# A hybrid decoder trunk on one Trainium2 core: query tiles ahead of the last gate tile, three half gate tiles in an attention's end, thirteen selection rounds moved

## The reference

```
h = RMSNorm(x) * (1 + scale) + shift              # scale, shift from c (adaLN)
z = h @ w_in                                      # all mixers' inputs and 4 x 1024 gate columns
A: gated convolution of width 3      D: sparse attention: an indexer scores all keys, each query
F: attention with forget biases         keeps its top 256, softmax over them with ALiBi
S: banded attention, window 128, sinks
y = sum over A, F, S, D of sigmoid(gate_n) * (branch_n @ w_branch_n)
x = x + g1 * RMSNorm(y @ w_o)
x = x + g2 * RMSNorm(SwiGLU(RMSNorm(x) ...))      # channel sub-layer
```

## Time and profile before

| | us |
|---|---|
| median of 3 runs | 1734.74 (1734.55 to 1738.4) |
| the profiled execution | 1735.29 |
| its span, first to last instruction | 1733.5 |
| PE busy | 1680.1 (97%) |
| DVE busy | 1055.2 (61%) |
| POOL busy | 822.4 (47%) |
| ACT busy | 613.3 (35%) |
| mean granted PE clock, share of full speed | 0.992 |

### The profile page before, as it was taken

One profiled execution on the slowest core, in us unless ns is written; L12 is line 12 of the kernel. 1 busy time (PEld: TensorE's weight loads), 2 busy tenths in 40 slices (PEclk: granted clock), 3 DMA queues, 4 the chain that ended last, 5 costly groups with the idle time before them and its releaser, 6 DMA issues.

```text
span 1733.5 us, 22877 instructions
## 1 busy us (share of the span) xinstructions
PE 1680.1 (97%) x8072; PEld 1397.3 (81%) x8072; DVE 1055.2 (61%) x1756; ACT 613.3 (35%) x1104; POOL 822.4 (47%) x537
## 2 busy tenths in 40 slices
PE   5999999999999999989999999999999999999997
PEld 4877878787888888879888888888888888888886
DVE  7745745556999999947486445843553454345337
ACT  5544336374222222246423455332223223222323
POOL 2421130102436565620288434675567656655755
PEclk9999999999999999999999999999999999999999
DMA  8131141010111111340575403120112012111205
GB/s 342 37 85 47 51 115 35 16 52 17 61 46 46 45 46 45 112 103 1 217 273 171 170 14 133 37 73 30 66 49 68 29 48 73 48 48 48 73 25 207
DMA packets 37455, 138.87 MB, mean 80 GB/s; under 512 B 4624, under 2 KB 4624, under 8 KB 37392
## 3 DMA queue, kind: packets, MB, share of 16 engines
q1 hardware_dynamic: 35152, 130.70, 21.7%
q0 software_dynamic: 2240, 7.34, 1.9%
HBM read 118.10 MB, written 13.63 MB: 76 GB/s over the span
## 4 chain that ended last, share of the span: by engine, by line
PE 68%; issue 11%; POOL 10%; DVE 4%; DMA 4%; ACT 2%; SPq 1%; POOLq 0%; ACTq 0%; DVEq 0%
PE ps L639 19%; PE ps L640 18%; PE ps L641 18%; POOL w_t L1713 5%; PE ps L863 4%; PE ps L842 2%; PE ps L766 1%; DMA raw<-in_w_ffn 1%; PE ps L767 1%; POOL w_f L1728 1%; DMA region_a<-in_x 1%; PE ps L670 1%; POOL raw L1731 1%; POOL slot_c L1713 1%; DVE region_c L1904 1%
## 5 line engine op out<-in xcount | busy, mean ns | idle before, releaser
L639 PE MATMUL ps<-h_t,w_t 128*128 128x512 f32 x1112 | 437.7, 394 | 3.3 <-DVE h_t L1896 1.6
L641 PE MATMUL ps<-h_t,w_t 128*128 128x512 f32 x1112 | 433.6, 390 | 0.0
L640 PE MATMUL ps<-h_t,w_t 128*128 128x512 f32 x1112 | 433.5, 390 | 0.0
L639 PEld LDWEIGHTS ps<-h_t,w_t 128*128 128x128 f32 x1112 | 209.4, 188 | 49.7 <-issue 5.5
L641 PEld LDWEIGHTS ps<-h_t,w_t 128*128 128x128 f32 x1112 | 209.1, 188 | 44.0
L640 PEld LDWEIGHTS ps<-h_t,w_t 128*128 128x128 f32 x1112 | 209.4, 188 | 42.8 <-issue 0.7
L1564 POOL TENSOR_TENSOR w_t<-raw,w_t 128x1280 fp32r<-128x1280 f32 (+1 forms) x50 | 145.9, 2918 | 198.2 <-ACT w_t L1154 197.9
L2265 DVE TENSOR_TENSOR y_f<-ps,y_f 128x512 f32<-128x512 f32 x120 | 80.7, 686 | 217.5 <-PE ps L641 217.5
L1713 POOL TENSOR_TENSOR w_t<-raw,w_t 128x512 fp32r<-128x512 f32 x80 | 110.2, 1383 | 136.7 <-ACT w_t L1452 136.7
L1950 DVE MAX8 top<-region_b 128x8 f32<-128x384 f32 (+5 forms) x192 | 157.9, 882 | 17.6 <-issue 17.0
L1953 DVE MATCH_REPLACE8 region_b<-top,region_b 128x384 f32<-128x384 f32 (+5 forms) x192 | 166.1, 876 | 0.0
(11 more groups left out here) (286 smaller groups left out, 3345.4 us busy)
## 6 DMA issues: line engine op xcount, KB each, us to landing
raw<-in_w_ffn SPq DMA_DIRECT2D x46, 512.0 KB, 3.9
raw<-in_w_gates SPq DMA_DIRECT2D x32, 640.0 KB, 3.9
region_b<-in_w_ada SPq DMA_DIRECT2D x33, 512.0 KB, 4.5
region_d<-in_w_ffn SPq DMA_DIRECT2D x20, 512.0 KB, 4.0
raw<-in_w_z SPq DMA_DIRECT2D x18, 512.0 KB, 3.4
region_a<-in_x SPq DMA_DIRECT2D x8, 512.0 KB, 14.9
h_f<-in_w_ada SPq DMA_DIRECT2D x8, 512.0 KB, 8.1
raw<-in_w_o SPq DMA_DIRECT2D x8, 512.0 KB, 3.6
```

The source lines that it names most:

```text
L639: pe.matmul(o, a_hi, m_hi, start=first, stop=False, skip_group_check=more)
L640: pe.matmul(o, a_hi, m_lo, start=False, stop=False, skip_group_check=more)
L641: return pe.matmul(o, a_lo, m_hi, start=False, stop=last, skip_group_check=more)
```

## The change

Four things are changed; what is computed stays the same.

1. `T_DSA` moves one place ahead. The order is now 23 gate tiles, the two query tiles, the last gate tile of branch S (`T_LAST`), the sparse attention. The queries' stacks move to the second buffer of `y_t`, and both low parts use one row of `region_c`; the other row holds the distances (`far`), since `region_d` is still in use. Branch D's results and products use buffer 0.
2. The banded attention's end is filled with three half gate tiles (`T_AFS`, and the first half of the next) in 12 parts, placed by `FILL`; the second half of that next tile is `gate_second`. Its weights are loaded in `w_t` during the second forget attention. For the sparse attention's end `FILL[2]` has the same places as before.
3. The spill of the last output columns gets its own semaphore; DVE and POOL wait for six spills, ACT for the last, before it writes `pt[1]`.
4. Thirteen rounds of block 5 (768 columns) run early on DVE: two behind the first convolution product, two behind `forget_spread(0)`, nine between the low parts of the tiles 9 to 12. The loop at the end runs 8 rounds over six blocks, 11 over five, 13 over four.

```diff
-T_DSA = T_AFS + 3 * KT
-T_GD = T_DSA + 2
+T_DSA = T_AFS + 3 * KT - 1
+T_LAST = T_DSA + 2
+T_GD = T_LAST + 1
+SIDE_BLOCK = 5
+SIDE_ROUNDS = {(0, 1): 2, (1, 0): 2, (2, 0): 2, (2, 1): 2, (3, 0): 1}
+FILL = {3: (1, 2, 2, 2, 3, 2), 2: (1, 1, 1, 1, 0, 1), 0: (0,) * 6}
...
+        far = region_c[:, L:2 * L]
-                  T_DSA: ("q", (ys[0], ys[1]), (lo_c[0], lo_c[0])),
-                  T_DSA + 1: ("q", (ys[2], ys[3]), (lo_c[1], lo_c[1]))}
+                  T_DSA: ("q", (ys[4], ys[5]), (lo_c[0], lo_c[0])),
+                  T_DSA + 1: ("q", (ys[6], ys[7]), (lo_c[0], lo_c[0]))}
...                                                               # SP
+            tile_load(T_DSA - 1, w_gates[3 * KT - 2])
             tile_load(T_DSA, w_z[T_AFS])
             tile_load(T_DSA + 1, w_z[T_AFS + 1])
-            for dt in range(1, KT):
+            sp.wait_ge(s_ys, 1)
+            sp.dma_start(far, distance).then_inc(s_table, 16)
+            tile_load(T_LAST, w_gates[3 * KT - 1])
+            def spill(dt, s):
                 sp.wait_ge(s_mix, MIX0 + 2 * (2 * KT + dt + 1))
-                sp.dma_start(mix_dram[:, dt, :], z[:, dt]).then_inc(s_spill, 16)
-            sp.dma_start(region_d[:, :], distance).then_inc(s_table, 16)
-            for j in range(2):
-                tile_load(T_GD + j, w_gates[3 * KT + j])
+                sp.dma_start(mix_dram[:, dt, :], z[:, dt]).then_inc(s, 16)
+            for dt in range(1, KT - 1):
+                spill(dt, s_spill)
+            tile_load(T_GD, w_gates[3 * KT])
+            spill(KT - 1, s_spill_last)
+            tile_load(T_GD + 1, w_gates[3 * KT + 1])
...                                                               # PE, attention
+                beside, parts_at = gates_beside(gate, halves), FILL[halves]
                     if u >= end - 2:
-                        next(beside)
+                        fill(parts_at[2 * (u - end + 2)])
                     if u - 2 >= u0:
                         turn_out(u - 2)
                     if u > u0:
                         values(u - 1)
                     if u >= end - 2:
-                        next(beside)
+                        fill(parts_at[2 * (u - end + 2) + 1])
+                fill(parts_at[4])
                 turn_out(end - 2)
                 values(end - 1)
-                next(beside)
+                fill(parts_at[5])
                 turn_out(end - 1)
-                for _ in beside:
-                    pass
+                fill(4 * KT)
+            def gate_half(bank, T, half):
+                for k in range(KT):
+                    c, w = slice(half * HALF, (half + 1) * HALF), slice(k * P, (k + 1) * P)
+                    product(ps[:, bank, :], w_t[:, T % 2, 0, w], w_t[:, T % 2, 1, w], h_hi[:, k, c], h_lo[:, k, c],
+                            k == 0, k == KT - 1)
+                    yield k
+            def gates_beside(T0, halves):
+                for n in range(halves):
+                    if n % 2 == 0:
+                        pe.wait_ge(s_w_lo, T0 + n // 2 + 1)
+                    for k in gate_half(4 + n, T0 + n // 2, n % 2):
                         if k % 2:
                             yield
...
-            attention(U_FOX + 2 * TT, 2 * TT + TT, T_AFS)
+            attention(U_FOX + 2 * TT, 2 * TT + TT, T_AFS, 3)
+            def gate_second(T, buf):
+                for _ in gate_half(7, T, 1):
+                    pass
+                for half in range(2):
+                    pe.wait_ge(s_zf, 2 * T + half - 1)
+                    tile_half(ps[:, 2 + half, :], T % 2, half, KT, BT, y_hi(buf), y_lo(buf)).then_inc(s_z, 1)
...                                                               # gate_tile
+                    if T == T_LAST:
+                        pe.wait_ge(s_z_lo, lo_halves(T_DSA + 1) + half + 1)
...
-            gate_tile(T_AFS + 1, 0)
+            gate_second(T_AFS + 1, 0)
...
-            gate_pairs(T_AFS + 2 * KT, 0)
-            z_group(T_DSA, T_GD - T_DSA)
+            gate_pairs(T_AFS + 2 * KT, 0, KT // 2 - 1)
+            gate_tile(T_DSA - 1, 0)
+            z_group(T_DSA, 2)
+            gate_tile(T_LAST, 0)
...                                                               # ACT, attention
+                    if gate is not None and u == u0 + 4:
+                        split_hi(gate + 1, n=GT)
+                    if u == U_DSA + 1:
+                        act.wait_ge(s_spill_last, 16)
...                                                               # POOL
+            split_lo(T_AFS + 1)
...
+            split_lo(T_DSA + 1)
+            stack_moves(T_DSA)
+            split_lo(T_LAST)
+            pool.wait_ge(s_key_out, 32)
+            pool.wait_ge(s_spill, 16 * (KT - 2))
+            for i, dst in enumerate((dsa_keys[0][0], dsa_keys[1][0])):
+                for half_rows in rows_of:
+                    pool.dma_start(dst[half_rows], key_dram[:, i, :]).then_inc(s_key_in, 16)
+            stack_moves(T_DSA + 1)
+            split_lo(T_GD)
+            gate_tile(T_LAST, KT - 1, False)
...                                                               # DVE
-                if T == T_FOX + 1 and half == 0:
-                    dve.wait_ge(s_moved[T_FOX], 32)
+                if T in (T_FOX + 1, T_DSA + 1) and half == 0:
+                    dve.wait_ge(s_moved[T - 1], 32)
...
+                if c == 0:
+                    top_k([SIDE_BLOCK], 2)
...
             forget_spread(0)
+            top_k([SIDE_BLOCK], 2)
             for T in range(T_FOX, T_SWA):
-                stack_lo(T)
-                if T == T_FOX + 1:
-                    forget_sums(0)
+                for half in range(2):
+                    stack_lo_half(T, half)
+                    if T == T_FOX + 1 and half:
+                        forget_sums(0)
+                    elif (T - T_FOX, half) in SIDE_ROUNDS:
+                        top_k([SIDE_BLOCK], SIDE_ROUNDS[T - T_FOX, half])
...
-            top_k(range(KB0, TT), rounds - rounds_done[KB0])
-            top_k(range(KB0 + 1, TT), rounds - rounds_done[TT - 1])
+            while any(n < rounds for n in rounds_done.values()):
+                left = [b for b in rounds_done if rounds_done[b] < rounds]
+                top_k(left, min(rounds - rounds_done[b] for b in left))
+            for T in range(T_DSA, T_LAST):
+                stack_lo(T)
             for b in range(KB0, TT):
                 order.mark(dve.tensor_scalar(sc_at[b], sc_at[b], TAKEN / 2, -BIG, ALU.is_gt, ALU.mult))
-            for T in range(T_DSA, T_GD):
-                stack_lo(T)
             order.wait()
             dve.wait_ge(s_table, 32)
-            dve.wait_ge(s_spill, 16 * (KT - 1))
+            dve.wait_ge(s_spill, 16 * (KT - 2))
             attention(U_DSA, HEADS * TT)
```

More of the change, by code:

```diff
@@ L251, in build @@
         stack_order = sorted(stacks)
-        wo_at = [(ys[2 * k], ys[2 * k + 1]) for k in range(4)] + [(wide_a[:, 2 * k], wide_a[:, 2 * k + 1]) for k in range(4)]
+        wo_at = [(ys[k], ys[k + 1]) for k in (4, 6, 0, 2)] + [(wide_a[:, 2 * k], wide_a[:, 2 * k + 1]) for k in range(4)]
         waste = w_t[:, :, :, D:GT]
@@ L493, in gate_tiles @@
         def gate_tiles(T):
-            return T_AFS <= T < T_DSA or T_GD <= T < T_WO
+            return T_AFS <= T < T_DSA or T_LAST <= T < T_WO
         def width(T):
@@ L876, in turn_out, with attention, fill @@
                 mm.then_inc(s_turned, 1)
-            def attention(u0, n, gate=None):
+            def attention(u0, n, gate=None, halves=0):
                 end = u0 + n
-                beside = gate_beside(gate)
+                beside, parts_at = gates_beside(gate, halves), FILL[halves]
+                def fill(parts):
+                    for _ in range(parts):
+                        next(beside, None)
                 logits(u0)
@@ L995, in column_sums @@
                     mm.then_inc(s_mod, 1)
-            gate_tile(T_WO - 1, 1, read=s_h_read, between=column_sums)
+            gate_tile(T_WO - 1, 0, read=s_h_read, between=column_sums)
             for k in range(KT):
@@ L1273, in group_hi @@
                 act.wait_ge(s_turned, g + 1)
-                dst, src = group_turned(u, y_hi(1))
+                dst, src = group_turned(u, y_hi(1 if units[u][0] == "fox" else 0))
                 act.activation(dst, src, ACT.Copy).then_inc(s_o_hi, 1)
@@ L1294, in exponentials, with attention @@
                                    accum_out=den[:, g % 4, col:col + 1]).then_inc(s_exp, 1)
-            def attention(u0, n):
+            def attention(u0, n, gate=None):
                 end = u0 + n
@@ L1319, in _ @@
             z_group(T_SWA, T_AFS - T_SWA)
-            attention(U_FOX + 2 * TT, 2 * TT + TT)
+            attention(U_FOX + 2 * TT, 2 * TT + TT, T_AFS)
             act.wait_ge(s_ya_in, 16 * BT)
@@ L1352, in mix_hi, with gate_pairs_begun @@
                 act.activation(h_hi[:, dt], z[:, dt], ACT.Copy).then_inc(s_mix_hi, 1)
-            def gate_pairs_begun(T0, m0, n=KT // 2):
```

(24 more changed lines are left out.)

50 lines of the change are left out of this document (17 added, 33 removed).

## The result

The changed kernel took 1722.88 us (median of four runs, 1721.94 to 1723.82), beside 1734.70 us for the kernel before: ratio 0.993, interval 0.9916 to 0.9944, 11.8 us less. The profiled execution took 1722.79 us (span 1721.0, mean clock 0.995), 12.5 us less than the one before.

What follows compares the result with a forecast made beforehand. TensorE (PE), busy 97% of the span, was taken to bound the kernel. 6.0 - 0.3 + 3.4 - 0.3 = 8.8 us off the 1734.7 median gave 1725.9, called 1726; range for 8 in 10: 1723 to 1731.5, own range 1723.5 to 1729.

Steps and rivals of the forecast that it cites:

- Part A: Banded attention's end: three half gate tiles fill PE's wait before the transposes; 6.0 us gained, from 2.5 to 6.9.
- early split: Second gate tile's weights, split by ACT and POOL in the forget attention's fifth unit: -0.3 us, between 0 and -1.5.
- Part B: Sparse attention's start: query tiles ahead of the last gate tile; 3.4 us gained, from 1.0 to 4.5.
- Part C: Thirteen block 5 rounds run early on DVE, at 2.4 us each: cost -0.3 us, from 0 to -1.5; gain 0.
- The wait of 3.5 and the low clock of 3.4 us: Banded attention's end: PE's wait before the transposes and the half clock after it both go, 3.5 and 3.4 us.
- the y_s copy: Banded attention's end: no part is left behind the last transposes, so PE's wait for this copy is bare, 0.7 us.
- Half of each: -1.1: Sparse start: half of a POOL-DVE clash (up to 1.4 us) and half of a low clock (about 1.4 us).
- even without the rounds moved nothing would be late. Gain 0.: Query tiles: DVE done at 732.80, the first low part needed at 736.8, so moving the rounds gains 0.
- One of its signs: Sign of being right: DVE's selection ends about 20 us before the query tiles.
- The new waits: Sparse start: last spill of mix with about 1 us margin, cost 0; T_LAST's halves and moves in time; third gate tile's weights 0.
- PE's idle time between 217 and 258 us: Sign of being wrong: more than 1 us of idle PE in this stretch.
- the rivals: Sparse start stays slow 1728.4 (16%); banded end keeps low clock 1729.4 (10%); both low 1731.8 (7%); rounds overrun 1737 (5%).

Runs made afterwards that it cites:

- fill_as_before: The changed kernel with three half gate tiles but the filling list placed as before, seven parts left behind the last transposes; 1729.47 us, ratio 0.997.
- queries_only: The changed kernel with two half gate tiles in the old places and no rounds moved, leaving the query tiles ahead of the last gate tile; 1729.89 us.
- banded_only: The kernel before with only the three half gate tiles, their filling list and early weight split, tile order kept; 1727.79 us, ratio 0.9958.
- no_rounds: The changed kernel with none of the thirteen rounds moved early; 1732.75 us, ratio 0.9994 to the kernel before.
- bias_early: The changed kernel with the banded attention's bias table loaded during the forget attention into the free weight buffer; 1720.97 us, ratio 0.9922.
- changed_again: The changed kernel, unedited, measured again beside the kernel before; 1725.30 us, ratio 0.995.

## Where the prediction held, and the step that failed

The ledger, against the profiled executions:

| term | forecast | measured |
|---|---|---|
| A, with the early split | 6.0 - 0.3 = 5.7 | 6.0 (6.7 alone) |
| B | 3.4 | 4.7 |
| C, its cost | -0.3 | -0.1 |
| last stage | none | 2.0 |
| sum | 8.8 | 12.5 |

Two terms took the time out of the range: part B, 1.3 us too small, and 2.0 us in the last stage, for which the sum had no term. With B alone put right the forecast is 1724.7, inside the range.

**Part A was right in mechanism and in size.** The wait of 3.5 and the low clock of 3.4 us go together (fill_as_before), the y_s copy stands bare at 0.56 us (0.7 forecast). The early split of the second gate tile cost nothing that shows: counted from the first logits of the second forget attention, PE's rows stand at the same place in both kernels to 0.01 us up to the banded attention's start. There the changed kernel waits 0.6 us longer (2.65 and 2.04 us); the same wait is 2.1 to 2.4 us in the seven other profiles that have it, with the early split and (queries_only, 2.4) without.

**Part B is the term that was mis-sized.** The step that failed is "Half of each: -1.1", the charge for a clash of POOL and DVE on the path and for a low clock. Nothing of it showed: the undisturbed sum of the forecast, 10.4 us, was within 0.15 us of the measured 10.25. (It was also added up wrong: half of 1.4 and half of 1.4 is 1.4, which would have made part B 3.1 and the forecast 1726.2.) The clash came, but to the engine that started later, and that was POOL, which had only the spill behind it. The Trainium skill (SBUF — State Buffer, "Who interferes with whom") says that the order of issue decides who blocks. The trace agrees, 1.27 us for the first and 2.14 for the second. The forecast had both outcomes of the clash, 4.5 and 3.1, and took a charge between them. The better way was to ask of the unlucky engine whether anybody waits for it: here the path's engine was the earlier by 0.27 us, in all eight profiles with this order (2.44 to 2.45 us behind the first logits, POOL's addition at 2.72 to 2.73). POOL's multiplication before it ended, by the profile, 0.20 us after DVE's bias had begun, and the bias shows 0.05 us of that. No run turned the order round, so what a late bias would have cost was not measured. With 4.5 in place of 3.4 the forecast is 1724.8. The low clock did not come at the short gaps of this start (0.42, 0.50 and 1.27 us) in any of the eight.

**Two microseconds were most likely not the change's.** This is the term that the sum lacked. In the kernel before, the profiled execution waits at branch D's third gate tile:

```profile
863.05 10.80 DVE L1801 SCALAR_TENSOR_TENSOR region_b<-region_b,silu_c 128x1024 f32<-128x1024 f32 x5 [3.07 <-DMA region_b<-in_w_ada]
...
863.11 4.00 POOL L1564 TENSOR_TENSOR w_t<-raw,w_t 128x1280 fp32r<-128x1280 f32 x1 [4.25 <-ACT w_t L1154]
...
867.24 0.49 PE L639 MATMUL ps<-h_t,w_t 128*128 128x512 f32 x1 [1.37 <-POOL w_t L1564]
```

and the changed kernel:

```profile
851.43 2.95 POOL L1610 TENSOR_TENSOR w_t<-raw,w_t 128x1280 fp32r<-128x1280 f32 x1 [2.82 <-ACT w_t L1191]
...
852.13 8.99 DVE L1857 SCALAR_TENSOR_TENSOR region_b<-region_b,silu_c 128x1024 f32<-128x1024 f32 x4 [2.33 <-DMA region_b<-in_w_ada]
```

In the first DVE starts 0.06 us ahead of POOL, and POOL's split of the weights takes 4.00 us; in the second POOL is first, and takes 2.95. The weights themselves had landed 1.2 us later too. Both streams are released by DMAs, and either can be first. PE's wait of 1.4 us is the larger part of the 2.0; the rest was not placed. The ten other profiles lack the wait, but only one of them, banded_only, has the old order; so that it was chance is argued from one profile with it and one without. Its row of 1.4 us stood in the list of waits, and whether it would repeat was not asked. How many of the runs behind the median of 1734.7 have it is open.

**Part C was wrong as an argument, and cost the sum nothing.** The step: "even without the rounds moved nothing would be late. Gain 0." It set the selection's end of the kernel before (732.80) against the date of the bank, 736.8, which was also the kernel before's, moved by B alone. Part A moves both (no_rounds): the date to 731.1, the selection's end to 736.1. The 4 us of slack became 5 us too little, and with DVE's own 1.4 us low part ahead of PE that is the 6.8 us of no_rounds. The rounds are worth 8.7 us; the forecast's sum is the same, because a wait that was not seen needed no cure in it. What the rounds cost was sized well: a round takes 2.40 us against 2.4, the second convolution product came 0.22 us later (207.19 for 206.97 in the earlier trace rows) against 0.25. One of its signs failed mostly for the same reason: DVE's selection was to end about 20 us before the query tiles, and it ended at 713.6, 6.5 us before they began. (The thirteen rounds took 22.4 us off its end, by no_rounds, for 24.5 forecast.)

**The new waits** stood as forecast: the spill lands 1.3 us before it is needed, and T_LAST, the moves and the third gate tile's weights hold nobody. PE's idle time between 217 and 258 us is 1.9 us, over the 1 us that was to be a sign of being wrong, but it was 1.9 us before the change as well. Of the rivals none happened. And of the miss against the medians (3.1 us) a part may be no miss at all: the second comparison of the same two kernels gave a ratio of 0.995, which is 8.7 us.

## What to carry to other kernels

When several moves go into one change, test the slack of each resource with all of them applied: a slack read from the old trace is worth nothing where one part brings the consumer forward and another holds the producer back. Find a low clock's price together with the wait that causes it, and place the filler by where the wait ends, not by how much of it there is. And when two kernels are compared by one profile each, cut both into stages of equal work: a stage that the change doesn't touch and that differs all the same wants more profiles before it is booked as gain or as chance, and here it was 2 of 12.5 us.

## What the runs showed of the hardware

The granted clock after an idle stretch of PE, in these kernels: after 6.8 us 0.62 for the next 5.2 us, after 3.4 us 0.57 for 8 us, after 3.3 us 0.64 for 4.8 us, after 2.65 us 0.54 in a stretch of 5 us, after the 1.3 us of the sparse start full. At the start of the first forget attention it differs from profile to profile: with the same wait of 1.74 us, the eight transposes behind it took 1.06 or 1.07 us in four profiles and 1.52 to 1.94 in seven, and the second stage came to between 77.7 us (mean granted clock 1.00) and 81.4 us (0.94), with 0.98 in the nine others. PE's windows of bias_early and of changed_again, which are alike there but for the chance:

```profile
262.00:266.00 4.00, 3.44 (x14) 0.50 0.00 0
266.00:270.00 4.00, 4.00 (x27) 0.73 0.02 4
```

```profile
262.00:266.00 4.00, 2.92 (x23) 1.00 0.00 0
266.00:270.00 4.00, 4.00 (x37) 1.00 0.01 4
```

So one kernel's executions differ by a few microseconds of clock. In the 28 runs of the kernel before that stand beside no_rounds, the longest (1740.7 us) has the lowest mean clock, 0.988, and the shortest (1730.8 us) the highest, 0.994; the two go together with a correlation of -0.83, so the clock is most of what a median has to average away here. Unexpected as well: a DVE operation on four columns was held for a whole POOL operation. It waited out 4.1 us of POOL's subtraction in the kernel before and 2.8 us in the changed one.
